# A mixture-of-experts kernel: a narrower all-token part of expert 0, its rows from one-hot products, and 64 slots on 64 array columns

## The chip, the cores and the metric

The kernel is written in Bass, with semaphores set by hand, and runs on one NeuronCore of a Trainium2 chip. The metric is the device time of one execution in microseconds (us).

## The reference

Two layers of an encoder on 256 tokens of 1024 values in float32. Each layer mixes tokens (one input projection; windowed attention on half of its columns, a pooling mixer on the other half; an output projection) and then channels. Layer 0 mixes channels with a dense SwiGLU, layer 1 with eight experts, of which each token takes two:

```python
D_MODEL, SEQ, DEPTH, D_FF, N_EXPERTS, TOP_K = 1024, 256, 2, 2816, 8, 2

def swiglu(t, w_gate, w_up, w_down):
    return (jax.nn.silu(t @ w_gate) * (t @ w_up)) @ w_down

def moe_swiglu(h, w_router, w_gate, w_up, w_down):
    t = h.reshape(B * S, Dm)
    logits = (t @ w_router).astype(jnp.float32)
    top_vals, top_idx = lax.top_k(logits, TOP_K)
    top_w = jax.nn.softmax(top_vals, axis=-1)
    gates = jnp.sum(jax.nn.one_hot(top_idx, N_EXPERTS) * top_w[..., None], axis=1)
    out = 0
    for e in range(N_EXPERTS):
        out = out + gates[:, e:e + 1] * swiglu(t, w_gate[e], w_up[e], w_down[e])
    return out

def reference(x, ...):
    for l in range(DEPTH):
        h = rms_norm(x, pre_mix_gain[l])
        y = ...                          # attention and pooling of h, times w_out[l]
        x = x + rms_norm(y, post_mix_gain[l])
        h = rms_norm(x, pre_ffn_gain[l])
        f_out = swiglu(h, ...) if l % 2 == 0 else moe_swiglu(h, ...)
        x = x + rms_norm(f_out, post_ffn_gain[l])
    return x
```

The expert weights are 8 x 3 x 1024 x 2816 values in float32, 277 MB; every expert is used, so all of them are read.

## The kernel before

**Experts.** The kernel computes an expert only for the tokens that chose it. Each expert has `SLOTS` = 96 slots for tokens: 64 form part A (`A_SLOTS`), 32 part B (`B_SLOTS`). The experts stand in an order of places p = 0 to 7; expert 0 is always at p = 0, the others are put in order by their number of tokens. `CAPS` gives each place 96 slots or 64: places 2 and 7 have part A alone (`has_b`). A round for tokens beyond the slots exists and is not entered with these inputs.

**TensorE in the expert stage.** The 2816 hidden columns of an expert are taken in three chunks c of 1024, 1024 and 768 columns (`width`, `col0`). The stationary operand is the tokens' rows (`xg`, turned so that the model dimension is on the partitions), the moving operand are the weights as they came from memory. A step of `gate_up` (L1996) is one k of eight: 128 rows of the gate or up weights times the width of the chunk. For part A it issues four matmuls on tiles of 128 rows and 32 columns of the array (L2011): two groups g of 32 slots, each with the two halves h of the chunk's columns. For part B it issues one matmul of 256 columns per 256 columns of the chunk (L2015), each on its own 32 array columns. `down` (L2041) has blocks of 128 hidden columns: four matmuls of 512 columns for A (L2064) and four of 256 for B (L2069), all on 32 array columns. So every matmul of both functions uses a tile `128*32`:

```python
for q in range(4):
    h, g = divmod(q, 2)
    last = pe.matmul(ps[tile(q), (B_GATE, B_UP)[part], 0:w // 2], xg[:, rows_at, k, tile(g)],
                     weights[:, h * w // 2:(h + 1) * w // 2], start=k == 0, stop=k == KT - 1)
if has_b(p):
    for q in range(w // FC):
        last = pe.matmul(ps[tile(q), (B_GATE_B, B_UP_B)[part], 0:FC], xg[:, rows_at, k, A_SLOTS:SLOTS],
                         weights[:, q * FC:(q + 1) * FC], start=k == 0, stop=k == KT - 1)
```

The order on TensorE is that of `experts` (L2102): for each place and chunk the gate steps, then the turning of the hidden rows of the chunk before (`turn_hidden`, L2026 for A and L2037 for B), the up steps, for c > 0 the turning of one half of the gathered rows of the next expert (`turn_picked`, L2099), and `down` of the chunk before. The turnings are transposes with an identity on TensorE. The last chunk's `down` follows behind early additions at the end.

**Loads.** SyncE's queue loads the weights in that order, in 280 pieces of up to 1 MB (`load_piece`: L831 for down, L836 for gate and up, two k to a piece) into a ring of 16 slots. A slot is loaded again when TensorE has counted the piece in it as used (`ring_used`). The first sixteen pieces take memory of the stages before: `RING_ORDER` lists the slots, and `first_use` (L808) what each waits for: the dense stage's down weights (n < 2), the attention (n < 4), the low parts of the first pieces (n < 8), then TensorE's last use of those pieces.

**Expert 0 in front.** So that TensorE has work while the tokens are routed, the first 512 hidden columns (`WIDE`) of expert 0 are computed for all 256 tokens. Their gate and up weights come in four pieces of two k (`load_first`, L799, `FIRST_PIECES`), each split by ScalarE and VectorE into a high and a low part (`split_first` at L1157 and L2283; for piece 2, `split_by_k`, L2275, in two halves). `all_piece(j, t)` (L1845) multiplies piece j with token tile t: for each of two k and of gate and up three products of 512 columns (`mm3`, L1541: high by high, low by high, high by low), so twelve matmuls a call, eight calls. `first_chunk` (L1866) sets the order: the products of token tile 0 (tokens 0 to 127), its router logits (`route`, L1813), the turning of the normalised rows of tile 1 (`turn_rows`, L1547, behind `post_norm` and `pre_norm` on VectorE, L2338 and L2310, and a square and a root on ScalarE), the router of tile 1 and the products of tile 1, with `find_places` (L1823) and `find_rows` (L1834) between them. VectorE turns the logits into one-hot matrices (`onehots`: token by slot). Expert 0's tokens then come in four steps: TensorE multiplies the one-hots with token numbers, VectorE copies the row (`tok_row`), GpSimdE gathers the rows from memory (`gather_picked`, L1050, out of `tok_dram`, where both tiles' rows were stored), and `turn_first` (L1882) turns them. `pick_hidden` (L1895) picks the hidden rows of expert 0's slots out of the all-token part by one-hot products on L1901, so that `down` of this part works on slots as elsewhere. The other 2304 columns of expert 0 are three chunks of 768.

The gather of a later place p + 2 waits until the rows of place p + 1 are turned. The space of the turned rows `xg` lies over `rows`, the normalised rows.

## Time and profile before

| what | value |
|---|---|
| three runs | 1048.09, 1048.44, 1050.11 us (median 1048.44) |
| profiled execution | 1048.1 us, span of its instructions 1046.3 us |
| TensorE clock granted, mean | 0.995 of full speed |
| instructions of TensorE | 9903 matmuls (transposes are matmuls too) |
| HBM read | 341 MB |
| layer 0 and the mixing of layer 1 | 0 to about 320 us |
| first steps on expert 0's slots | 364.6 us |

```text
span 1046.3 us, 22297 instructions
## 1 busy us (share of the span) xinstructions
PE 1022.9 (98%) x9903; PEld 578.9 (55%) x9903; DVE 270.5 (26%) x418; ACT 250.7 (24%) x426; POOL 54.3 (5%) x159
## 2 busy tenths in 40 slices
PE   8999999999999899999999999999999999999985
PEld 7987888888998654444433334444444444443321
DVE  7677545446677410000000000000000000000022
ACT  7766534344775200000000000000000000000021
POOL 4000000000101000001001000001001000100200
PEclk9999999999999999999999999999999999999998
DMA  8488556542638899999999999999999999999994
GB/s 290 175 264 275 195 175 201 186 160 97 213 112 299 293 366 361 420 418 359 397 420 408 419 418 408 418 419 401 399 419 419 402 419 419 406 418 418 418 406 166
DMA packets 125149, 347.24 MB, mean 332 GB/s; under 512 B 7368, under 2 KB 40176, under 8 KB 125056
## 3 DMA queue, kind: packets, MB, share of 16 engines
q1 hardware_dynamic: 119760, 331.64, 82.0%
q0 software_dynamic: 4560, 13.41, 3.8%
q8 instruction: 76, 1.25, 0.4%
q10 hardware_dynamic: 736, 0.80, 0.2%
q14 instruction: 17, 0.14, 0.0%
HBM read 341.10 MB, written 4.72 MB: 331 GB/s over the span
## 4 chain that ended last, share of the span: by engine, by line
PE 93%; DMA 3%; DVE 2%; issue 1%; SPq 1%; ACT 1%; DVEq 0%; ACTq 0%; POOLq 0%
PE ps L2011 29%; PE ps L2064 14%; PE ps L2015 10%; PE ps L1543 9%; PE ps L1545 9%; PE ps L1544 9%; PE ps L2069 5%; DMA ring<-in_moe_w_down 2%; PE ps L2026 1%; DMA gains<-tok_rows,tok_row 1%; PE ps L2099 1%; DMA raw_gu<-in_w_in 1%; SPq L831 0%; PE ps L1550 0%; PE ps L1932 0%
## 5 line engine op out<-in xcount | busy, mean ns | idle before, releaser
L2011 PE MATMUL ps<-ring,xg 128*32 128x512 f32 (+1 forms) x3072 | 380.0, 550 | 2.6 <-DMA ring<-in_moe_w_gate 1.6
L2064 PE MATMUL ps<-ring,moe_ht 128*32 128x512 f32 x1408 | 177.3, 593 | 2.7 <-DMA ring<-in_moe_w_down 2.7
L2015 PE MATMUL ps<-ring,xg 128*32 128x256 f32 x2048 | 176.2, 379 | 0.0
L2011 PEld LDWEIGHTS ps<-ring,xg 128*32 128x32 f32 x3072 | 110.6, 110 | 99.7 <-issue 47.3
L2015 PEld LDWEIGHTS ps<-ring,xg 128*32 128x32 f32 x2048 | 73.2, 110 | 146.6 <-issue 146.6
L1543 PE MATMUL ps<-hi_gu,xt_hi 128*128 128x512 f32 (+1 forms) x352 | 132.3, 376 | 1.3 <-DVE lo_gu L2257 1.1
L1545 PE MATMUL ps<-hi_gu,xt_lo 128*128 128x512 f32 (+1 forms) x352 | 129.1, 367 | 0.0
L1544 PE MATMUL ps<-lo_gu,xt_hi 128*128 128x512 f32 (+1 forms) x352 | 129.0, 367 | 0.0
L1438 ACT ACTIVATE moe_silu<-ps 128x512 f32<-128x512 f32 (+1 forms) x24 | 13.3, 553 | 333.8 <-PE ps L2015 275.3
L2701 DVE COPY moe_ht<-ps 128x256 f32<-128x256 f32 (+1 forms) x18 | 7.1, 394 | 295.5 <-PE ps L2037 295.5
L2069 PE MATMUL ps<-ring,moe_ht 128*32 128x256 f32 x1056 | 81.2, 379 | 0.0
L2711 DVE TENSOR_TENSOR moe_hidden<-moe_silu,ps 128x512 f32<-128x512 f32 (+1 forms) x24 | 15.2, 632 | 255.2 <-PE ps L2015 189.1
L2069 PEld LDWEIGHTS ps<-ring,moe_ht 128*32 128x32 f32 x1056 | 34.3, 110 | 79.0 <-issue 79.0
L1543 PEld LDWEIGHTS ps<-hi_gu,xt_hi 128*128 128x128 f32 x352 | 66.6, 189 | 13.6 <-issue 1.2
L1545 PEld LDWEIGHTS ps<-hi_gu,xt_lo 128*128 128x128 f32 x352 | 66.6, 189 | 11.1
L1544 PEld LDWEIGHTS ps<-lo_gu,xt_hi 128*128 128x128 f32 x352 | 66.7, 190 | 9.9
L2064 PEld LDWEIGHTS ps<-ring,moe_ht 128*32 128x32 f32 x1408 | 43.8, 110 | 50.8 <-issue 24.3
L2197 DVE TENSOR_TENSOR lo_gu<-raw_gu,hi_gu 128x2048 fp32r<-128x2048 f32 x24 | 54.7, 2283 | 2.9 <-ACT hi_gu L1100 2.1
L1456 ACT COPY xg<-ps 128x384 f32<-128x384 f32 (+1 forms) x16 | 7.2, 452 | 135.1 <-PE ps L2099 135.1
L1100 ACT CAST hi_gu<-raw_gu 128x2048 fp32r<-128x2048 f32 x20 | 38.2, 1908 | 0.0
L1058 POOL DMA_DIRECT2D y_rows<-y_sb x14 | 7.6, 545 | 580.7 <-ACT y_sb L1463 580.7
L2518 DVE TENSOR_TENSOR lo_d<-raw_d,hi_d 128x1024 fp32r<-128x1024 f32 x20 | 23.6, 1221 | 31.4 <-ACT hi_d L1377 31.4
(326 smaller groups left out, 879.5 us busy)
## 6 DMA issues: line engine op xcount, KB each, us to landing
ring<-in_moe_w_down SPq DMA_DIRECT2D x88, 1024.0 KB, 16.5
ring<-in_moe_w_gate SPq DMA_DIRECT2D x56, 1024.0 KB, 17.6
ring<-in_moe_w_up SPq DMA_DIRECT2D x56, 1024.0 KB, 17.9
ring<-in_moe_w_gate SPq DMA_DIRECT2D x40, 768.0 KB, 15.3
ring<-in_moe_w_up SPq DMA_DIRECT2D x40, 768.0 KB, 14.2
raw_gu<-in_dense_w_gate SPq DMA_DIRECT2D x22, 512.0 KB, 3.9
raw_gu<-in_dense_w_up SPq DMA_DIRECT2D x22, 512.0 KB, 4.9
raw_d<-in_dense_w_down SPq DMA_DIRECT2D x11, 1024.0 KB, 4.9
```

Source lines behind the costliest of these rows:

```text
L1100: act.copy(hi_gu[at], raw_gu[at]).then_inc(gu_hi_done, 1)
L1438: last = act.activation(moe_silu[:, 0:w // 2], ps[:, B_GATE, 0:w // 2], ACT.Silu)
L1543: pe.matmul(o, a_hi, b_hi, start=first, stop=False)
L1544: pe.matmul(o, a_hi, b_lo, start=False, stop=False)
L1545: return pe.matmul(o, a_lo, b_hi, start=False, stop=last)
L2011: last = pe.matmul(ps[tile(q), (B_GATE, B_UP)[part], 0:w // 2], xg[:, rows_at, k, tile(g)], weights[:, h * w // 2:(h + 1) * w // 2], start ...
L2015: last = pe.matmul(ps[tile(q), (B_GATE_B, B_UP_B)[part], 0:FC], xg[:, rows_at, k, A_SLOTS:SLOTS], weights[:, q * FC:(q + 1) * FC], start=k ...
L2064: last = pe.matmul(ps[tile(q), B_YA, :], moe_ht[:, at:at + 32], weights[:, h * 512:(h + 1) * 512], start=start, stop=stop)
L2069: last = pe.matmul(ps[tile(q), B_YB, 0:FC], moe_ht[:, at:at + 32], weights[:, q * FC:(q + 1) * FC], start=start, stop=stop)
L2197: dve.tensor_tensor(lo_gu[at], raw_gu[at], hi_gu[at].bitcast(F32), ALU.subtract).then_inc(gu_lo_done, 1)
L2518: dve.tensor_tensor(lo, raw_d[:, c % 2, k, :], hi.bitcast(F32), ALU.subtract).then_inc(d_lo_done, 1)
L2711: last = dve.tensor_tensor(moe_hidden[:, 0:w // 2], moe_silu[:, 0:w // 2], ps[:, B_UP, 0:w // 2], ALU.mult)
```

## The change

The part of expert 0 that is computed for all tokens has 256 hidden columns instead of 512. It comes in two pieces of four k, gate and up side by side in one product of 512 columns; pieces 2 and 3, their splits on ScalarE and VectorE and their loads are gone. The rest of expert 0 has chunks of 1024, 1024 and 512 columns; in the last, B's groups are 128 wide and a piece has four k. The two slots of memory that become free, and the four behind them, come earlier in `RING_ORDER`. Expert 0's rows are no longer gathered: `pick_rows` multiplies the rows of all tokens with the one-hot matrix on TensorE, which gives them turned at once. For this `xg` no longer lies over `rows`. Part A is issued as two matmuls on 64 array columns (`half_tile`), one for each half of the chunk's columns, instead of four on 32. Part B stays on 32.

```diff
-B_LOGITS, B_PLACES, B_COUNTS, B_ALL, B_XG0 = 4, 4, 7, ((0, 1), (5, 6)), (3, 7)
+B_LOGITS, B_PLACES, B_COUNTS, B_ALL, B_XG0 = 4, 4, 7, (0, 5), (3, 7)
...
-    FIRST_PIECES = 4
+    FIRST_PIECES = 2
...
-    RING_ORDER = [4, 5, 14, 15] + [first_slot(j) for j in range(FIRST_PIECES)] + \
+    EARLY_SLOTS = [first_slot(j) for j in range(FIRST_PIECES, 4)]
+    RING_ORDER = [4, 5, 14, 15] + EARLY_SLOTS + [base + n for n in EARLY_SLOTS for base in (6, 10)] + \
+        [first_slot(j) for j in range(FIRST_PIECES)] + \
         [base + first_slot(j) for j in range(FIRST_PIECES) for base in (6, 10)]
...
     def width(p, c):
 
         if c < 0:
-            return WIDE
-        return 3 * FC if p == 0 or c == CHUNKS - 1 else 4 * FC
+            return FC
+        if c < CHUNKS - 1:
+            return 4 * FC
+        return 3 * FC if p else 2 * FC
 
     def col0(p, c):
 
         if c < 0:
             return 0
-        return WIDE + c * 3 * FC if p == 0 else c * 4 * FC
+        return c * 4 * FC + (0 if p else FC)
+
+    def b_width(p, c):
+        return P if width(p, c) == 2 * FC else FC
+
+    def b_groups(p, c):
+        return width(p, c) // b_width(p, c)
+
+    def k_tiles(p, c):
+
+        return 2 if width(p, c) > 2 * FC else 4
+
+    def gate_pieces(p, c):
+        return KT // k_tiles(p, c)
...
         if c < 0:
             return b * SLOTS + A_SLOTS
-        q, j = divmod(b, 2)
+        q, j = divmod(b, b_width(p, c) // P)
         return 512 + j * P + q * B_SLOTS
...
+    def half_tile(h):
+        return slice(A_SLOTS * h, A_SLOTS * (h + 1))
...
-                to = flat_piece(raw_gu, slot).rearrange("p (k w c) -> p k w c", k=2, w=2)
+                to = flat_piece(raw_gu, slot).rearrange("p (k w c) -> p k w c", k=4, w=2)
                 for part, w in enumerate((moe_w_gate, moe_w_up)):
-                    sp.dma_start(to[:, :, part, :], w[0, 0][2 * j * P:(2 * j + 2) * P, 0:WIDE]
+                    sp.dma_start(to[:, :, part, :], w[0, 0][4 * j * P:(4 * j + 4) * P, 0:FC]
                                  .rearrange("(k p) n -> p k n", p=P)).then_inc(gu_loaded[slot // 2][slot % 2], 16)
 
             def first_use(n):
@@ -811,10 +828,14 @@
                     sp.wait_ge(d_lo_done, 2 * NCH)
                 elif n < 4:
                     sp.wait_ge(attn_mm, TT * DEPTH)
-                elif n < 8:
-                    sp.wait_ge(gu_lo_done, PIECE0 + n - 4 + 1)
...
+                elif n < 6:
+                    sp.wait_ge(gu_lo_done, PIECE0)
+                elif n < 10:
+                    sp.wait_ge(out_mm, TT * DEPTH)
+                elif n < 12:
+                    sp.wait_ge(gu_lo_done, PIECE0 + n - 10 + 1)
                 else:
-                    sp.wait_ge(first_used, (n - 8) // 2 + 1)
+                    sp.wait_ge(first_used, (n - 12) // 2 + 1)
...
                 else:
-                    w, c0 = width(p, c), col0(p, c)
-                    sp.dma_start(ring[:, slot, 0:2 * w].rearrange("p (k n) -> p k n", k=2),
-                                 expert_rows((moe_w_gate, moe_w_up)[part], e)[i * FC:(i + 1) * FC, c0:c0 + w]
+                    w, c0, kn = width(p, c), col0(p, c), k_tiles(p, c)
+                    sp.dma_start(ring[:, slot, 0:kn * w].rearrange("p (k n) -> p k n", k=kn),
+                                 expert_rows((moe_w_gate, moe_w_up)[part], e)[i * kn * P:(i + 1) * kn * P, c0:c0 + w]
                                  .rearrange("(k p) n -> p k n", p=P)).then_inc(ring_loaded[slot], 16)
...
             pool.wait_ge(tok_stored, 16 * TT)
             pool.wait_ge(tok_row_ready, 1)
-            gather_picked(0)
-            pool.wait_ge(tok_row_ready, 2)
-            pool.wait_ge(picked_turned, 2)
             gather_picked(1)
...
                 transposed(l, T_FFN, 0)
                 split_first(l, 1)
                 post_mix(l, 1)
-                split_first(l, 2)
                 pre_ffn(l, 1)
-                split_first(l, 3)
                 transposed(l, T_FFN, 1)
...
-            def all_piece(j, t, between=None):
+            def all_piece(j, t):
 
                 hi, lo = flat_piece(hi_gu, first_slot(j)), flat_piece(lo_gu, first_slot(j))
                 a = slice(t * P, (t + 1) * P)
-                for k in range(2):
-                    kt = 2 * j + k
-                    if (j, t, k) == (2, 0, 0):
-                        pe.wait_ge(first_k_lo, 1)
-                    elif t == 0:
-                        pe.wait_ge(gu_lo_done, PIECE0 + j + 1)
-                    if k and between:
-                        between()
-                    for part in range(2):
-                        at = slice((2 * k + part) * WIDE, (2 * k + part + 1) * WIDE)
-                        last = mm3(ps[:, B_ALL[t][part], :], xt_hi[:, kt, a], xt_lo[:, kt, a], hi[:, at], lo[:, at],
-                                   kt == 0, kt == KT - 1)
+                if t == 0:
+                    pe.wait_ge(gu_lo_done, PIECE0 + j + 1)
+                for k in range(4):
+                    kt, at = 4 * j + k, slice(k * WIDE, (k + 1) * WIDE)
+                    last = mm3(ps[:, B_ALL[t], :], xt_hi[:, kt, a], xt_lo[:, kt, a], hi[:, at], lo[:, at], kt == 0, kt == KT - 1)
                 if t == 1:
                     last.then_inc(first_used, 1)
-                elif j == 3:
+                elif j == FIRST_PIECES - 1:
                     last.then_inc(all_tile0, 1)
 
             def first_chunk():
                 all_piece(0, 0)
-                all_piece(1, 0)
                 pe.wait_ge(router_lo_done, 1)
                 route(0)
-                all_piece(2, 0)
                 turn_rows(1, T_FFN, 1)
-                all_piece(3, 0)
+                all_piece(1, 0)
                 xt_ready(1, T_FFN, 1)
                 route(1)
                 all_piece(0, 1)
                 find_places()
-                all_piece(1, 1, lambda: find_rows(0, range(1)))
-                all_piece(2, 1)
-                all_piece(3, 1, turn_first)
-
-            def turn_first():
-                pe.wait_ge(counted, 1)
+                all_piece(1, 1)
                 for part in range(2):
-                    turn_picked(0, part)
+                    pick_rows(part)
+
+            def pick_rows(part):
+                pe.wait_ge(*((counted, 1) if part else (onehots_ready, 1)))
+                for k in range(4):
+                    at = slice((part * 4 + k) * P, (part * 4 + k + 1) * P)
+                    for t in range(TT):
+                        last = pe.matmul(ps[:, B_XG0[part], k * SLOTS:(k + 1) * SLOTS], rows[:, t, at],
+                                         onehots[:, t, 0, 0:SLOTS].bitcast(F32), start=t == 0, stop=t == TT - 1)
+                last.then_inc(picked_turned, 1)
...
+                for k in range(2):
...
@@ -1998,23 +2009,24 @@
...
-                    pe.wait_ge(*((all_silu, 1) if part == GATE else (all_hidden, 1)))
+                    pe.wait_ge(all_hidden, 1 if part == GATE else TT)
...
+                kn = k_tiles(p, c)
                 for k in range(KT):
-                    slot = piece_ring(p, c, part, k // 2)
-                    if k % 2 == 0:
-                        pe.wait_ge(ring_loaded[slot], piece_level(p, c, part, k // 2, step))
-                    weights = ring[:, slot, (k % 2) * w:(k % 2 + 1) * w]
-                    for q in range(4):
-                        h, g = divmod(q, 2)
-                        last = pe.matmul(ps[tile(q), (B_GATE, B_UP)[part], 0:w // 2], xg[:, rows_at, k, tile(g)],
+                    slot = piece_ring(p, c, part, k // kn)
+                    if k % kn == 0:
+                        pe.wait_ge(ring_loaded[slot], piece_level(p, c, part, k // kn, step))
+                    weights = ring[:, slot, (k % kn) * w:(k % kn + 1) * w]
+                    for h in range(2):
+                        last = pe.matmul(ps[half_tile(h), (B_GATE, B_UP)[part], 0:w // 2], xg[:, rows_at, k, 0:A_SLOTS],
                                          weights[:, h * w // 2:(h + 1) * w // 2], start=k == 0, stop=k == KT - 1)
                     if has_b(p):
-                        for q in range(w // FC):
-                            last = pe.matmul(ps[tile(q), (B_GATE_B, B_UP_B)[part], 0:FC], xg[:, rows_at, k, A_SLOTS:SLOTS],
-                                             weights[:, q * FC:(q + 1) * FC], start=k == 0, stop=k == KT - 1)
-                    if k % 2:
+                        wb = b_width(p, c)
+                        for q in range(b_groups(p, c)):
+                            last = pe.matmul(ps[tile(q), (B_GATE_B, B_UP_B)[part], 0:wb], xg[:, rows_at, k, A_SLOTS:SLOTS],
+                                             weights[:, q * wb:(q + 1) * wb], start=k == 0, stop=k == KT - 1)
+                    if k % kn == kn - 1:
                         last.then_inc(ring_used, 1)
...
                     weights = ring[:, slot, (b % 2) * D:(b % 2 + 1) * D]
                     start, stop = first and b == 0, end and b == width(p, c) // P - 1
-                    for q in range(4):
-                        h, g = divmod(q, 2)
-                        at = a_at(p, c, b) + 32 * g
-                        last = pe.matmul(ps[tile(q), B_YA, :], moe_ht[:, at:at + 32], weights[:, h * 512:(h + 1) * 512],
+                    for h in range(2):
+                        at = a_at(p, c, b)
+                        last = pe.matmul(ps[half_tile(h), B_YA, :], moe_ht[:, at:at + A_SLOTS], weights[:, h * 512:(h + 1) * 512],
                                          start=start, stop=stop)
...
             def turn_picked(p, part):
-                b, cap = B_XG0[part] if p == 0 else B_XG, CAPS[p]
-                pe.wait_ge(picked_loaded, p * 16 + 16)
-                if p:
-                    pe.wait_ge(xg_ready, 2 * p + part)
-                    if has_b(p - 1):
-                        pe.wait_ge(ht_b_ready, b_chunk_of(p - 1, part) + 1)
+                cap = CAPS[p]
+                pe.wait_ge(picked_loaded, p * 16)
+                pe.wait_ge(xg_ready, 2 * p + part)
+                if has_b(p - 1):
+                    pe.wait_ge(ht_b_ready, b_chunk_of(p - 1, part) + 1)
                 for k in range(4):
                     at = slice((part * 4 + k) * P, (part * 4 + k + 1) * P)
-                    last = pe.transpose(ps[:, b, k * cap:(k + 1) * cap], picked[0:cap, at], ident[0:cap, 0:cap])
+                    last = pe.transpose(ps[:, B_XG, k * cap:(k + 1) * cap], picked[0:cap, at], ident[0:cap, 0:cap])
                 last.then_inc(picked_turned, 1)
...
             def split_first(l, j):
-                if l and j == 2:
-                    split_by_k(j)
-                elif l:
+                if l:
                     split_first_piece(j)
...
                 post_norm(l, POST_MIX, 1, banks(B_OUT[1], 2))
-                split_first(l, 2)
                 pre_norm(l, PRE_FFN, 1)
-                split_first(l, 3)
...
                 link(dve.tensor_scalar(slot[:], rank[:], NOT_CHOSEN, None, ALU.add))
-                dve.wait_ge(tok_row_mm, 1)
-                dve.tensor_copy(tok_row[:, 0:1], ps[:, B_PLACES, 8 * E:8 * E + 1]).then_inc(tok_row_ready, 1)
```

Left out are the same widths put into the copies, the SiLU and the products of the hidden rows, the memory of `xg`, and the counts of semaphores.

## Rows read from the trace of the kernel before

**Rows 1.** The page, busy time and instructions of each engine.

```profile
PE 1022.9 (98%) x9903; PEld 578.9 (55%) x9903; DVE 270.5 (26%) x418; ACT 250.7 (24%) x426; POOL 54.3 (5%) x159
```

**Rows 2.** Window; PE, PEld, DVE, ACT, POOL busy us; clock; DMA share; GB/s.

```profile
318.00:400.00 82.00, 77.96 (x647) 53.58 (x645) 32.74 (x71) 21.58 (x30) 3.60 (x5) 0.98 0.90 322
500.00:957.00 457.00, 457.00 (x5461) 188.60 (x5457) 21.42 (x46) 28.30 (x61) 17.98 (x31) 1.00 1.03 413
```

**Rows 3.** TensorE's timeline: start of a group, its length, line, form, records.

```profile
454.09 0.61 PE L2015 MATMUL ps<-ring,xg 128*32 128x256 f32 x8
454.63 0.55 PE L2026 MATMUL ps<-ident,moe_hidden 128*128 128x128 f32 x3
455.02 0.33 PE L2037 MATMUL ps<-ident,moe_hidden 96*128 96x96 f32 x2
455.28 1.06 PE L2011 MATMUL ps<-ring,xg 128*32 128x512 f32 x8
...
700.50 1.04 PE L2011 MATMUL ps<-ring,xg 128*32 128x512 f32 x8
701.36 0.61 PE L2015 MATMUL ps<-ring,xg 128*32 128x256 f32 x8
701.79 1.04 PE L2011 MATMUL ps<-ring,xg 128*32 128x512 f32 x8
```

**Rows 4.** The chain from 995 us to the end, in order of time.

```profile
1001.48 0.95 SPq L836
...
1008.04 16.74 DMA ring<-in_moe_w_down
...
1029.08 5.33 PE ps L2064 x48
```

**Rows 5.** The windows view, a stretch of layer 0's dense stage.

```profile
100.00:150.00 50.00, 50.00 (x228) 41.37 (x227) 24.87 (x21) 20.98 (x21) 0.00 (x0) 1.00 0.63 201
```

**Rows 6.** Around the first experts' start: timelines, one step of chain, one window.

```profile
335.60 2.35 DVE L2281 TENSOR_TENSOR lo_gu<-raw_gu,hi_gu 128x1024 fp32r<-128x1024 f32 x2
338.06 1.28 DVE L2310 SCALAR_TENSOR_TENSOR rows<-x_res,rstd,gains 128x1024 f32<-128x1024 f32 x1
...
344.97 0.11 PE ps L1820
...
360.79 1.47 PE L2099 MATMUL ps<-ident,gains 96*128 96x96 f32 x8 [3.98 <-DMA gains<-tok_rows,tok_row]
...
360.80:364.30 3.50, 3.50 (x14) 2.97 (x14) 0.00 (x0) 0.96 (x2) 0.00 (x0) 0.51 1.03 417
...
374.92 2.00 PE L1901 MATMUL ps<-onehots,y_sb 128*128 128x96 f32 x16
```

**Rows 7.** Durations by line (ns: least, median, most), first and last start.

```profile
L2011 PE MATMUL ps<-ring,xg x3072: 485/592/617, 364.6 to 1015.9; 128*32 128x512 f32 x112, 128*32 128x384 f32 x80
...
L1698 PE MATMUL ps<-k_t,q_t x64: 269/269/320, 35.7 to 291.1; 64*64 64x128 f32 x64
...
L2026 PE MATMUL ps<-ident,moe_hidden x86: 272/273/330, 400.2 to 1027.0; 128*128 128x128 f32 x86
```

**Rows 8.** TensorE's timeline in the attention of layer 1, columns as in rows 3.

```profile
289.81 0.50 PE L1693 MATMUL ps<-k_t,q_t 64*128 64x128 f32 x6
290.24 0.45 PE L1698 MATMUL ps<-k_t,q_t 64*64 64x128 f32 x8
...
305.51 0.22 PE L1717 MATMUL ps<-v_mid,probs 128*64 128x65 f32 x1
305.57 0.22 PE L1717 MATMUL ps<-v_mid,probs 128*64 128x65 f32 x1
```

**Rows 9.** Groups by line and form: busy us, mean ns; idle before.

```profile
L2015 PE MATMUL ps<-ring,xg 128*32 128x256 f32 x2048 | 176.2, 379 | 0.0
L2069 PE MATMUL ps<-ring,moe_ht 128*32 128x256 f32 x1056 | 81.2, 379 | 0.0
```

More of the change, by code:

```diff
@@ L177, in build_trunk @@
             for part in (GATE, UP):
-                for i in range(4):
+                for i in range(gate_pieces(p, c)):
                     PIECE[p, c, part, i] = len(PIECE)
@@ L214, in piece_level @@
         if slot < 4:
-            earlier = first_level([first_slot(j) for j in range(FIRST_PIECES)].index(slot))
+            earlier = first_level([first_slot(j) for j in range(4)].index(slot) - (4 if slot in EARLY_SLOTS else 0))
         else:
@@ L224, in last_piece @@
     def last_piece(p, c, part, step=None):
-        i = 3 if part != DOWN else width(p, c) // FC - 1
+        i = gate_pieces(p, c) - 1 if part != DOWN else width(p, c) // FC - 1
         return piece_number(p, c, part, i, step) + 1
@@ L872, in _ @@
                     for part in (GATE, UP):
-                        for i in range(4):
+                        for i in range(gate_pieces(p, c)):
                             if (p, c, part) != (0, 0, GATE) or i >= 2:
@@ L1439, in silu_of @@
                 if has_b(p):
-                    some = b_rows(p, c)
-                    last = act.activation(moe_silu[some, 512:3 * FC], ps[some, B_GATE_B, 0:FC], ACT.Silu)
+                    some, wb = b_rows(p, c), b_width(p, c)
+                    last = act.activation(moe_silu[some, 512:512 + wb], ps[some, B_GATE_B, 0:wb], ACT.Silu)
                 last.then_inc(silu_ready, 1)
@@ L1450, in copy_picked_ht @@
                 act.wait_ge(hidden_picked, 1)
-                act.copy(moe_ht[:, 0:4 * SLOTS], ps[:, B_HTA, 0:4 * SLOTS]).then_inc(picked_ht_ready, 1)
+                act.copy(moe_ht[:, 0:2 * SLOTS], ps[:, B_HTA, 0:2 * SLOTS]).then_inc(picked_ht_ready, 1)
             def copy_xg(p, part):
@@ L1832, in find_places, with find_rows @@
                 last.then_inc(counts_mm, 1)
-            def find_rows(n, some):
-                pe.wait_ge(onehots_ready, n + 1)
-                for e in some:
+            def find_rows():
+                pe.wait_ge(onehots_ready, 2)
+                for e in range(1, E):
                     for t in range(TT):
@@ L1897, in pick_hidden @@
                 pe.wait_ge(all_hidden, TT)
-                for k in range(4):
+                for k in range(2):
                     at = slice(k * P, (k + 1) * P)
@@ L2035, in turn_hidden @@
                     some = b_rows(p, c)
-                    for j in range(2):
+                    for j in range(b_width(p, c) // P):
                         last = pe.transpose(ps[:, B_HTB, j * P:j * P + some.stop], moe_hidden[some, 512 + j * P:512 + (j + 1) * P],
@@ L2045, in down @@
                     pe.wait_ge(picked_ht_ready, 1)
[L2046 removed]
+                    pe.wait_ge(tok_row_ready, 1)
                 else:
@@ L2108, in experts @@
                         if (p, c) == (0, 0):
-                            find_rows(1, range(1, E))
+                            find_rows()
                             pick_hidden()
@@ L2273, in copy_q @@
                                   ).then_inc(q_copied, 1)
-            def split_by_k(j):
-                slot_at = first_slot(j)
-                dve.wait_ge(gu_hi_done, PIECE0 + j + 1)
-                for k in range(2):
-                    raw, hi, lo = (flat_piece(ring, slot_at)[:, k * 2 * WIDE:(k + 1) * 2 * WIDE] for ring in (raw_gu, hi_gu, lo_gu))
-                    dve.tensor_tensor(lo, raw, hi.bitcast(F32), ALU.subtract).then_inc(gu_lo_done if k else first_k_lo, 1)
             def split_first(l, j):
-                if l and j == 2:
-                    split_by_k(j)
-                elif l:
+                if l:
                     split_first_piece(j)
```

34 lines of the change are left out of this document (16 added, 18 removed).

## The prediction

> **What bounds the kernel now.** I first read the page's busy shares and then one table over time. TensorE is busy 98% of the span [rows 1]. From 500 to 957 us it has no idle time, while the DMA engines are full at 413 GB/s [rows 2], so the expert stage is held from two sides at nearly the same rate. One step of the stage (128 rows of gate or up weights, 1024 columns) takes 0.86 us for the first 64 slots (part A, L2011) and 0.43 us for the other 32 (part B, L2015) [rows 3]. That is 1.29 us, or 2.58 us for the two steps that use up one piece of 1.05 MB, which is 407 GB/s. TensorE is the slower side, by 1.5%. The two experts without a part B need 1.72 us for a piece and live on what the ring holds. For the last of them that does not suffice: the chain is TensorE's until 1001 us and then goes over the issue of the last transfers and a transfer of 16.74 us [rows 4].
>
> How much do these waits cost? From 1001.25 us, TensorE's remaining work is 16 steps of 768 columns (0.86 x 3/4 = 0.645 us), four pieces of down weights at 1.72, turns and early additions of 3.1, and the last three pieces in 5.33 [rows 4]: 25.7 us, to 1026.95. It really ends at 1034.4. So 7.4 us are DMA waits, which vanish if TensorE becomes slower before that point.
>
> **The change, part by part.** *Narrower all-token part.* For each token tile, each of four pieces was a block of 12 products, 50/228 = 0.22 us apart [rows 5]; here, with small gaps, I take 0.23, so 2.75 us a block. Only two pieces are left. I count from the rows of token tile 1, which both kernels need. VectorE ends them at 339.34 us, behind two subtractions of 2.35 us that the change removes [rows 6]. What then holds is ScalarE's square and root of that tile, and 0.65 us of the 2.35 are gained: 338.7. Before, the experts begin at 364.6 [rows 7], 25.3 us after the rows. After, TensorE does from 338.7 on: eight turns at (455.02 - 454.63)/3 = 0.13 [rows 3], 1.0, three blocks 8.25, 16 router and 5 place products at 0.11 [rows 6] = 2.3, and the new one-hot products, and then waits for one copy of 0.65 us that nothing hides. The new products have the form of L1901 (16 records in 2.00 us [rows 6], 0.112 apart): 32 records, 3.6 us. Together 15.8, so the experts begin at 354.5. I take 354.6, 10.0 us earlier. Gone from the 25.3 us are two blocks, the wait of 3.98 us for the gathered rows and their turning in 1.47 [rows 6], and what the half clock behind that wait costs (granted 0.51, the lower of the two levels, 1.2 GHz [rows 6]). Picking the hidden rows halves (1.0 us less). The 14 records that find the other experts' rows stay.
>
> There is a price in front: TensorE, through with its first block and the router at about 334.9, waits for the rows until 338.7. An idle stretch of 3.98 us was followed by half the clock [rows 6], so 3.8 us may be too. Bound: 0 to 1.8 us; I take 0, since it would fall partly under the following chain on ScalarE and VectorE.
>
> *Columns moved.* Expert 0 had 48 gate/up steps of 768 columns, 0.645 + 0.43 = 1.075 us each: 51.6 us. Now it has 32 of 1024 (1.29) and 16 of 512 (0.43 + 0.215): 51.6 us. The down blocks are 22 in both. This costs nothing. The bytes are the same as well: 2.1 MB move from the first loads to the ring.
>
> *Loads.* On SyncE's queue the two freed slots and the four behind them open early, so up to 8 MB can be under way before 340 us. DMA moves 322 GB/s from 318 to 400 us and 413 when it is full [rows 2]. Hence it has room for 82 x (1 - 322/413) = 18 us of transfers and can follow a gain of 11 us. GpSimdE's queue loses one gather, and the one for expert 1 no longer waits for expert 0's turning: needed at about 400 us, hidden either way. In sum so far: -11.0 us.
>
> *64 columns of the array at once.* Part A goes from four matmuls on 32 array columns to two on 64. Four streams of 512 columns side by side take 0.86 us; two streams of the same length take the same if two really run together. They do: on tiles 128*64, pairs start 0.06 us apart for 65 columns [rows 8], which is one stream's time for two. So A itself gains nothing. But B stays on tiles 128*32. Before, A and B had one form; now each step changes form twice.
>
> What a change of form costs is in the trace. The last B record ends at 454.70 and lasts 379 ns [rows 9], so it starts at 454.32; it streams 0.213 us, to 454.535, and the first record of the form 128*128 starts at 454.63. The way back is the same: the last turn ends at 455.35 and, with 96 columns, lasts 0.25 (273 ns for 128 columns [rows 7], less 0.03 of streaming), so it starts at 455.10 and streams 0.08, and the form 128*32 starts at 455.28 [rows 3]. A third change alters only the array's columns, from 64*128 to 64*64: the last pair (end 290.31, length 0.27) starts at 290.04 and streams 0.107, the next starts at 290.24 [rows 8]. Each leaves 0.095 us empty. Then the weights are loaded in sight: the first records last 617 instead of 592 ns for 32 columns, and 320 instead of 269 for 64 [rows 7], so 0.025 and 0.051. Third, everything waits for the last of the side-by-side tiles, which start 0.007 us apart: 0.02 with four, 0.007 with two. Hence A to B costs 0.127 us and B to A 0.166.
>
> How often? Six of the eight experts have a part B, each with 48 gate/up steps and 22 down blocks: 420 steps (L2069's 1056 records are 132 blocks of eight [rows 9]; L2015's 2048 belong to 288 steps). So 420 times A to B is 53.3 us. B to A is 389 times, 64.6 us, because 31 steps (18 gate chunks before a turn of hidden rows, 12 up chunks before a turn of gathered rows, one before the last one-hots) end before work on 128 columns, where the change exists already. Another 40 returns from such work go to 64 columns instead of 32, 1.0 us. Together 119 us, all on TensorE, which is the bound here.
>
> No row changes between 64 and 32 columns, so the bounds are wider: below, no cost at all; above, the dearest change seen (at 454.63: 0.54 us after 454.09 where a B group takes 0.43 [rows 3], so 0.11 late, and 330 instead of 273 ns [rows 7] for the load, 0.06: 0.17) each time, 138 us. I take 119, since the nearest row, 64*128 to 64*64, also changes columns alone. The Trainium skill has a rule on this ("TensorEngine Tiling (Array Packing)", Key Properties): changing the tiling mode, not just the tile, drains TensorE. By that rule the 119 us come; the same list says that different tiles load and multiply in parallel, and if that covered tiles of two widths they would not.
>
> **The sum.** Span 1046.3 - 11.0 (first part) - 7.4 (waits at the end that go) + 119 = 1147 us. Around the span lie 1.8 us (1048.1 less 1046.3), so 1148.7, say **1149 us**. The profiled execution is 0.3 us below the median of 1048.44. What becomes late next is nothing but TensorE: at 1.29 + 0.293 = 1.58 us a step a piece lasts 3.2 us against 1.05/0.413 = 2.5 for its transfer, and the ring is full when each narrow expert starts.
>
> **The rivals.**
> *No cost of the change of form.* If tiles of 64 and 32 columns share the array as tiles of one width do, only the 11 us remain. Then DMA sets the end as now, but started earlier: 1048.1 - 11 = 1037 us. For it: column tiles overlap freely within one form. Against it: all forms that follow each other in the trace leave 0.095 us. It decides from 11 + 7.4 us of added TensorE time, 0.044 us a step: below that the kernel is faster. Chance 0.12.
> *Only the loads are exposed.* The array isn't emptied, but weights of another width can't be loaded ahead: 420 x 0.025 + 389 x 0.051 + 1 = 31 us. TensorE is the bound, 1048.1 - 18.4 + 31 = 1061 us. For it: the loads of 454.63 are not pulled ahead. Against it: they come 0.095 us after the stream, not at once. Chance 0.07.
> *Cost in full*, the forecast: 0.80. What is left, 0.01, is no change.
>
> **How the numbers follow.** The forecast's own range: 809 changes at the bare 0.095 us are 77 us, which gives 1107; at 0.171 us they are 138, which gives 1168; the clock in front adds up to 1.8. So 1106 to 1168, and this already holds 8 in 10; the two rivals lie outside. Differences within 0.2% are about what can't be told from none here: same 0.02, faster 0.12, slower 0.86.
>
> **What the profile should show.** Forecast: L2011 and L2064 as 128*64 with half the records (1536 and 704), and a step of 1.58 us where it was 1.29; idle gaps on TensorE with no releaser, about 0.1 us, twice a step; DMA below 350 GB/s in the steps of B experts; experts starting near 354.6 us; DMA no longer in the chain's end. The gather's wait of 3.98 us is gone, and an idle stretch of about 3.8 us stands near 335. I am wrong if the step stays at 1.29 us (then 1037), or if a step of A alone, in the experts without B, is not 0.86 us, which would mean that two tiles of 64 don't run together for 512 columns.

## The result, and the profile after

The changed kernel takes 1149.51 us (median of 4 runs, 1148.61 to 1150.95) against 1048.26 us before in the same comparison: a ratio of 1.0965, 95% interval 1.0947 to 1.0982. The forecast was 1149. The profiled execution is the longest of the four, 1150.95 us with a span of 1148.3. One of the six executions of e4_group_all below had a granted clock of 0.942, where all others had 0.99 or more, and took 1074.8 us; it is left out of every comparison.

Of the page, busy time by engine [rows 1], the lines for part A and part B, and the last line of TensorE in the chain:

```profile
PE 1129.0 (98%) x7725; PEld 510.9 (44%) x7725; DVE 265.6 (23%) x414; ACT 246.7 (21%) x424; POOL 53.3 (5%) x158
...
L2022 PE MATMUL ps<-ring,xg 128*64 128x512 f32 (+2 forms) x1536 | 364.9, 572 | 0.6 <-ACT xg L1472 0.6
L2075 PE MATMUL ps<-ring,moe_ht 128*64 128x512 f32 x704 | 181.3, 611 | 0.0
L2027 PE MATMUL ps<-ring,xg 128*32 128x256 f32 (+1 forms) x2144 | 180.1, 385 | 0.0
...
L2080 PE MATMUL ps<-ring,moe_ht 128*32 128x256 f32 x1056 | 84.3, 391 | 0.0
```

Part A (L2022, L2075) has half the records that it had before (L2011, L2064), and TensorE is busy for 106 us longer. It is 98% busy before and after: the share says nothing here, since the roughly 0.1 us in which nothing streams at a change lie inside the duration of the last records (a record of 256 columns lasts 0.379 us and streams for 0.213). One has to look at the starts. TensorE's timeline of one step in expert 0, to be read against [rows 3]:

```profile
359.97 1.08 PE L2022 MATMUL ps<-ring,xg 128*64 128x512 f32 x4
360.98 0.64 PE L2027 MATMUL ps<-ring,xg 128*32 128x256 f32 x8
361.55 0.65 PE L2022 MATMUL ps<-ring,xg 128*64 128x512 f32 x2
```

A takes 360.98 - 359.97 = 1.01 us where it took 0.86, B 0.57 where it took 0.43. The step is 1.58 us, as forecast, against 1.29. What a record lasts shows the part of it that is weight loading: the durations (least, median, most) of the two lines are

```profile
L2022 PE MATMUL ps<-ring,xg x1536: 379/592/644, 358.4 to 1121.6; 128*64 128x512 f32 x128, 128*64 128x384 f32 x56, 128*64 128x256 f32 x8
...
L2027 PE MATMUL ps<-ring,xg x2144: 272/379/403, 359.4 to 1052.1; 128*32 128x256 f32 x184, 128*32 128x128 f32 x11
```

The median of both is that of before, 592 and 379 ns. Only the longest, those behind a change, last 0.052 and 0.024 us more. There the new weights are not loaded ahead: the loads for this B begin at 360.97 us, together with its first product at 360.98, while in the kernel before the loads for the B group at 454.09 us began at 453.66. In an expert without part B nothing changes width, and there the wide tiles cost nothing. The timeline has one such group (its first record may lie outside the window):

```profile
600.41 3.17 PE L2022 MATMUL ps<-ring,xg 128*64 128x512 f32 x13
```

Thirteen records are six pairs and one. Less the 0.59 of the last record, six pairs start in 2.58 us, 0.43 a pair, 0.86 for the two pairs of a step.

The windows, to be read against [rows 2] and the last view of [rows 6]:

```profile
336.70:340.40 3.70, 0.12 (x2) 0.03 (x1) 2.12 (x3) 1.45 (x3) 0.53 (x1) 0.68 1.02 417
340.60:344.80 4.20, 4.20 (x14) 3.71 (x15) 1.19 (x1) 2.21 (x2) 0.54 (x1) 0.50 1.01 340
344.90:350.80 5.90, 5.90 (x35) 5.13 (x34) 2.07 (x9) 0.30 (x2) 0.00 (x0) 1.00 1.01 395
500.00:957.00 457.00, 457.00 (x3302) 120.24 (x3298) 18.33 (x39) 24.79 (x53) 14.00 (x24) 1.00 0.97 358
```

From 500 to 957 us TensorE again has no idle time, but the DMA engines move 358 GB/s instead of 413, because the slots of the ring come free later: SyncE's queue waits for TensorE in 333 of these 457 us, where it was 134. From 400 to 500 us, where both experts have a part B, it is 306 GB/s (forecast: below 350). In front of the experts TensorE is idle for 3.7 us, and the clock then stands at 0.50 (1.2 GHz) until about 344.8. The waits say what it was idle for; no wait for a transfer is left in the list, where before there were 2.7 us at L2064 alone:

```profile
PE ps L1566 <- DVE rows L2310: 3.7, 1, 3.7
...
PE ps L2022 <- ACT xg L1472: 0.6, 1, 0.6
```

### The profile page after: what moved, and what is told of

Same layout as the page of the kernel before. It is cut to its first block, busy times and chain, and to the rows that moved or that the text cites. A ratio compares the mean times of both kernels' runs of the same rounds, so it can differ in the third digit from the quotient of the medians.

```text
span 1148.3 us, 17922 instructions
## 1 busy us (share of the span) xinstructions
PE 1129.0 (98%) x7725; PEld 510.9 (44%) x7725; DVE 265.6 (23%) x414; ACT 246.7 (21%) x424; POOL 53.3 (5%) x158
## 4 chain that ended last, share of the span: by engine, by line
PE 94%; DVE 2%; DMA 2%; ACT 1%; issue 1%; SPq 0%; DVEq 0%; ACTq 0%
PE ps L2022 30%; PE ps L2075 15%; PE ps L2027 14%; PE ps L1559 8%; PE ps L1561 7%; PE ps L1560 7%; PE ps L2080 7%; DMA raw_gu<-in_w_in 2%; PE ps L2038 1%; PE ps L2109 1%; PE ps L1566 1%; PE ps L1943 0%; PE ps L1733 0%; PE ps L1752 0%; PE ps L1741 0%
## 5 line engine op out<-in xcount | busy, mean ns | idle before, releaser
L2022 PE MATMUL ps<-ring,xg 128*64 128x512 f32 (+2 forms) x1536 | 364.9, 572 | 0.6 <-ACT xg L1472 0.6
L2075 PE MATMUL ps<-ring,moe_ht 128*64 128x512 f32 x704 | 181.3, 611 | 0.0
L2027 PE MATMUL ps<-ring,xg 128*32 128x256 f32 (+1 forms) x2144 | 180.1, 385 | 0.0
L2022 PEld LDWEIGHTS ps<-ring,xg 128*64 128x64 f32 x1536 | 83.8, 135 | 157.3 <-issue 155.9
L2027 PEld LDWEIGHTS ps<-ring,xg 128*32 128x32 f32 x2144 | 44.8, 108 | 209.8 <-issue 209.8
L1454 ACT ACTIVATE moe_silu<-ps 128x512 f32<-128x512 f32 (+2 forms) x24 | 13.4, 558 | 404.5 <-PE ps L2027 341.4
L2698 DVE COPY moe_ht<-ps 128x256 f32<-128x256 f32 (+2 forms) x18 | 7.2, 398 | 360.5 <-PE ps L2049 360.5
L2708 DVE TENSOR_TENSOR moe_hidden<-moe_silu,ps 128x512 f32<-128x512 f32 (+2 forms) x24 | 15.3, 638 | 291.2 <-PE ps L2027 228.9
L2075 PEld LDWEIGHTS ps<-ring,moe_ht 128*64 128x64 f32 x704 | 38.6, 135 | 74.2 <-issue 72.7
L2080 PEld LDWEIGHTS ps<-ring,moe_ht 128*32 128x32 f32 x1056 | 20.8, 108 | 107.1 <-issue 107.1
```

Source lines behind the costliest of these rows:

```text
L1454: last = act.activation(moe_silu[:, 0:w // 2], ps[:, B_GATE, 0:w // 2], ACT.Silu)
L2022: last = pe.matmul(ps[half_tile(h), (B_GATE, B_UP)[part], 0:w // 2], xg[:, rows_at, k, 0:A_SLOTS], weights[:, h * w // 2:(h + 1) * w // 2] ...
L2027: last = pe.matmul(ps[tile(q), (B_GATE_B, B_UP_B)[part], 0:wb], xg[:, rows_at, k, A_SLOTS:SLOTS], weights[:, q * wb:(q + 1) * wb], start=k ...
L2075: last = pe.matmul(ps[half_tile(h), B_YA, :], moe_ht[:, at:at + A_SLOTS], weights[:, h * 512:(h + 1) * 512], start=start, stop=stop)
L2080: last = pe.matmul(ps[tile(q), B_YB, 0:FC], moe_ht[:, at:at + 32], weights[:, q * FC:(q + 1) * FC], start=start, stop=stop)
L2708: last = dve.tensor_tensor(moe_hidden[:, 0:w // 2], moe_silu[:, 0:w // 2], ps[:, B_UP, 0:w // 2], ALU.mult)
```

## The experiments

Ten kernels ran. The first four were compared with each other and with before (median 1048.37) on one chip.

**Part A back on 32 columns (e1_a32).** The inverse of the diff's edit in `gate_up` and `down`, all else as changed:

```diff
-                    for h in range(2):
-                        last = pe.matmul(ps[half_tile(h), ...], xg[:, rows_at, k, 0:A_SLOTS],
+                    for q in range(4):
+                        h, g = divmod(q, 2)
+                        last = pe.matmul(ps[tile(q), ...], xg[:, rows_at, k, tile(g)],
```

> The changed kernel with part A back on four matmuls on 128*32 tiles; everything else of the change stays (256 all-token columns, one-hot products for the rows, chunks of 1024, 1024, 512, the earlier loads). Theory (each change of the tile's width costs 0.10 us on TensorE before and about 0.04 us behind it, nothing else of the change costs): the step is 1.29 us again and the whole added time of 108 us in the expert stage goes; the front part keeps its gain, of which about 2 us are eaten by the half clock behind the idle stretch at 337 us, so 1037 to 1041 us. Rival (the loss comes from the new chunks, the piece of four k or the loads at SyncE): it stays well above 1048 us, at 1060 to 1149 us.

Measured: 1039.09 us (1037.67 to 1043.82), ratio to before 0.9924, interval 0.9895 to 0.9952. The 64-column tiles alone cost 110.4 us, more than the whole loss of 101.3, and the rest of the change gains 9 us. Its chain, in order of time from 330 us on, has the transfers of [rows 4] back:

```profile
993.42 1.57 SPq L852
995.18 1.59 SPq L852
996.96 16.74 DMA ring<-in_moe_w_down
1013.74 1.92 PE ps L2077 x16
1017.98 5.33 PE ps L2077 x48
```

**The kernel before with part A on 64 columns (e2_before_a64).** The same edit the other way round, in the kernel before.

> The kernel before with one edit: part A as two matmuls on 128*64 tiles. Same columns, loads, gather. Theory: the same 420 changes 64 to 32 and 389 back, 0.288 us a step: step 1.575 us, plus 117 us, less the 7.4 us of transfer waits near the end that it covers: 1156 to 1161 us. Rival (two wide tiles are cheap and the loss lies elsewhere in the change): 1048 us or a little less.

Measured: 1157.43 us (1156.96 to 1160.25), ratio 1.1043, interval 1.1019 to 1.1067, so 109.1 us more. Both ways the price of the tiles is the same within 1.3 us, hence it doesn't come from the new chunks, the loads or the front.

**Fewer changes of width (e3_group_piece).** In the changed kernel the products stay the same and only their order changes. `group` is the number of k that one piece holds, for `down` two blocks:

```diff
-                for k in range(KT):
...
+                for k0 in range(0, KT, group):
+                    for b_part in range(2 if has_b(p) else 1):
+                        for k in range(k0, k0 + group):
```

> The changed kernel with the same products in another order: within each loaded piece all of part A first, then all of part B, so the width changes twice a piece instead of twice a step. Theory (the price hangs on the number of changes): changes 64 to 32 fall from 420 to 206, changes back from 389 to 175, 62 us less: 1085 to 1090 us, two steps in 2.87 us. Rival (a product on a 128*64 tile or the narrow product beside it is itself slower): unchanged, 1149 us. Rival (only the weight loads show): the same fall of about half, but without the empty 0.1 us at each remaining change.

Measured: 1088.4 us (1087.34 to 1089.2), 61.1 less. The timeline of one piece:

```profile
361.07 1.94 PE L2031 MATMUL ps<-ring,xg 128*64 128x512 f32 x8
362.94 1.07 PE L2027 MATMUL ps<-ring,xg 128*32 128x256 f32 x16
363.94 1.94 PE L2031 MATMUL ps<-ring,xg 128*64 128x512 f32 x8
```

Two steps in 2.87 us, as expected: A has 1.87 against 1.72, B 1.00 against 0.86. The excess at each change is what it was, 0.15 and 0.14 us; there are half as many. The fall of 61.1 us over 214 pairs of changes is 0.286 us for a pair. That this 0.14 to 0.15 us remains at each change refutes the rival by which only the loads show (0.024 and 0.052 us).

**All of A, then all of B (e4_group_all).** `group` is the whole chunk.

> The changed kernel with all of part A of a chunk's gate, up or down first and then all of part B: 55 changes 64 to 32 and 24 back are left. Theory: 107 us less by TensorE's count, 1042 us; a piece is given back only in the part B pass, so the ring holds up to four pieces longer and the DMA engines, which then bound the stage, may lose some: 1040 to 1050 us. Rival (price not by the number of changes): near 1149 us.

Measured: 1045.51 us (median of five executions, 1044.57 to 1046.82), ratio 0.9961, interval 0.9942 to 0.998. With 420 - 55 = 365 and 389 - 24 = 365 changes fewer each way, 0.286 us a pair make 104.4; measured are 104.0. Three points (0, 214 and 365 pairs fewer) lie on one line. TensorE's waits on transfers are only 0.7 us, so holding the ring's slots longer cost next to nothing. My 1042 was low since I had used 0.293 a pair.

**Two widths on separate columns (e9_mixed_halves, with e10_one_width_halves as control).** Does a change wait only where the new tile lies over a busy one? Here each wide product on one half of the array is followed by narrow ones on the other half. The wide product behind them then lies on the same columns as they do, so that the run answers the question for the step from 64 columns to 32, not for the way back.

```diff
                     for h in range(2):
...
-                    if has_b(p):
...
-                        for q in range(b_groups(p, c)):
...
+                        if has_b(p):
...
+                            for q in range(2 * (1 - h), min(2 * (2 - h), b_groups(p, c))):
...
```

> The changed kernel with the gate and up products of a step in the order: part A's first half of columns on array columns 0 to 63 (tile 128*64), part B's groups on columns 64 to 127 (tiles 128*32), part A's second half on 64 to 127, part B's groups on 0 to 63. down is as in the changed kernel. The two widths never want the same array columns at the same time. Theory (a change of width empties the whole array, wherever the tiles lie): the four phases of a step run one after the other, 0.86 + 0.43 + 0.86 + 0.43 = 2.58 us and four changes of 0.144, 3.15 us a step; with 344 us of added streaming and 83 us of added changes, 1576 us. Rival (only tiles that overlap wait for each other, so tiles of two widths run side by side): the step falls towards 1.3 to 1.7 us and the time to 1066 to 1180 us.

> The same order of halves as in e9_mixed_halves, but part A on tiles 128*32 throughout, as a control: one width, no change. It shows what the order itself costs. If tiles of one width run freely beside each other, a step takes 1.29 us (each half of the array has 0.86 + 0.43 us of work) and the time is 1039 us; if the queue hands them out strictly in order, so that a second pass on a tile holds those behind it, up to 1.72 us a step, 1039 + 288 x 0.4 = 1155 us; if neighbouring groups don't overlap at all, 2.58 us, 1390 us.

Measured: 1566.88 us for the two widths and 1039.88 us for the control in one run each, beside 1045.76 for the kernel before. The timeline with two widths:

```profile
403.31 1.07 PE L2022 MATMUL ps<-ring,xg 128*64 128x512 f32 x2
404.31 0.63 PE L2027 MATMUL ps<-ring,xg 128*32 128x256 f32 x4
404.87 1.07 PE L2022 MATMUL ps<-ring,xg 128*64 128x512 f32 x2
405.87 0.62 PE L2027 MATMUL ps<-ring,xg 128*32 128x256 f32 x4
406.43 1.07 PE L2022 MATMUL ps<-ring,xg 128*64 128x512 f32 x2
```

and the same order with one width:

```profile
403.20 0.39 PE L2028 MATMUL ps<-ring,xg 128*32 128x256 f32 x2
403.22 0.60 PE L2023 MATMUL ps<-ring,xg 128*32 128x512 f32 x2
403.42 0.39 PE L2028 MATMUL ps<-ring,xg 128*32 128x256 f32 x2
403.63 0.60 PE L2023 MATMUL ps<-ring,xg 128*32 128x512 f32 x2
403.65 0.60 PE L2028 MATMUL ps<-ring,xg 128*32 128x256 f32 x4
404.06 0.61 PE L2023 MATMUL ps<-ring,xg 128*32 128x512 f32 x4
```

Each product is two records (part A's 768 products in `gate_up` are L2022's 1536 records), called its first and second pass here. With one width the first pass of B (403.20) and the second pass of A (403.22) start together, by the order of the program on different halves, and the step is 1.29 us. With two widths the phases follow one another, 1.56 us each (403.31 to 404.87), two a step: 3.12 us. The narrow products at 404.31 and 405.87 us do not wait for their own columns: those were free during the whole wide product before. So at a change from 64 columns to 32 nothing starts before the wide products are through, wherever the tiles lie. That the same holds from 32 to 64 is not shown by this run; the change costs about as much either way (0.15 and 0.14 us above). This is the rule that the prediction cited from the Trainium skill ("TensorEngine Tiling (Array Packing)", Key Properties): changing the mode, not just the tile, drains TensorE. The 1576 us of the expectation follow from it; this case's trace agrees as far as it goes, with 1566.9 us and 3.12 us a step where 3.15 were expected. The other line of that list in the Trainium skill, that different tiles load and multiply in parallel, holds here within one width, where the control's step is 1.29 us.

The next four were compared on one chip with before at 1047.77 us. The base:

> The kernel of e1_a32 once more, as the base that the next three are compared with on one chip: 1039 us, as there.

Measured: 1039.27 us (1038.09 to 1041.44), ratio 0.9926, interval 0.9913 to 0.9939.

**Filling the idle stretch (e6_a32_fill).** `fill` issues 15 products of `xt_hi[:, 0, 0:P]` by 512 columns of piece 0 into the bank `B_UP`, which is not in use yet.

```diff
                 route(0)
+                fill(15)
                 turn_rows(1, T_FFN, 1)
```

> e1_a32 with 15 products of 512 columns into an unused bank in the place where TensorE waits 3.7 us for the rows of tile 1; the reference needs none of them. Theory (that idle stretch is what halves the clock for 6.8 us behind it): the granted clock stays at its full level from 337 us on, the eight turns take 0.9 instead of 1.97 us and the five or six products behind them 0.23 instead of 0.43, so the experts begin 2.2 us earlier and the time falls by as much, to 1036.5 to 1037.5 us. Rival (the clock falls for another reason, or the transfers set the end and take the 2 us back): 1039 us.

Measured: 1036.94 us (1036.38 to 1038.23), ratio 0.9901, interval 0.9887 to 0.9916. The windows before and behind the arrival of the rows:

```profile
335.00:338.70 3.70, 3.70 (x17) 2.72 (x16) 2.12 (x3) 1.45 (x3) 0.54 (x1) 1.00 1.02 418
338.90:343.00 4.10, 4.10 (x25) 3.60 (x25) 1.23 (x1) 2.30 (x2) 0.54 (x1) 1.00 1.03 344
```

and the timeline, turning and the first expert step:

```profile
338.89 1.10 PE L1566 MATMUL ps<-ident,rows 128*128 128x128 f32 x8 [0.18 <-DVE rows L2319]
...
354.72 1.06 PE L2030 MATMUL ps<-ring,xg 128*32 128x512 f32 x8 [0.57 <-ACT xg L1472]
```

The clock stays at full. The turning begins at 338.89 us, exactly as in the profile of e1_a32 (338.89), and the experts at 354.72 instead of 357.11: 2.4 us from the clock alone, and the time falls by 2.3. The seven profiled executions with this front and the idle stretch have 17.39 to 18.57 us from the turning to the experts, this one 15.83, so the half clock costs 1.6 to 2.7 us.

**The one-hot products alone (e7_before_onehot_rows),** put into the kernel before:

```diff
             def turn_first():
-                pe.wait_ge(counted, 1)
                 for part in range(2):
-                    turn_picked(0, part)
+                    pick_rows(part)
```

with the memory of `xg` moved and expert 0's gather, number product and copy left out, as in the change.

> The kernel before with one part of the change alone: expert 0's rows from one-hot products on TensorE instead of the gather and the turning; still 512 all-token columns in four pieces, chunks of 768, part A on 32 columns. Theory: the wait of 4.0 us, the turning of 1.5 and about 1.0 of half clock behind the wait go, 3.6 us of products come: the experts begin 2.9 us earlier, 1045 to 1046.5 us. The narrower all-token part and the earlier loads are then worth the other 6 us of the 9 that e1_a32 gained. Rival (the gather was hidden for the most part, and the products only add): 1048 to 1052 us.

Measured: 1044.64 us (12 runs, 1042.8 to 1048.2), ratio 0.9971, interval 0.996 to 0.9983: 3.1 us less, 0.4 below the expected range. The experts begin at 361.25 us instead of 364.6, 3.3 us earlier (expected 2.9). The clock behind the products, where [rows 6] had 0.51:

```profile
355.00:361.00 6.00, 6.00 (x45) 5.49 (x43) 0.61 (x4) 0.96 (x2) 0.00 (x0) 1.00 1.02 408
```

So 3.1 of the 8.5 us that e5_a32_again gains come from the rows. The rest is put down to the narrower part and the earlier loads, which were not run alone.

**The front packed more closely (e8_best).** `all_piece(1, 0)` in two halves around the turning, with 9 and 4 filling products, and `pick_rows` ahead of the last k of `all_piece(1, 1)`:

```diff
+                all_piece(1, 0, range(2))
+                fill(9)
                 turn_rows(1, T_FFN, 1)
-                all_piece(1, 0)
+                all_piece(1, 0, range(2, 4))
+                fill(4)
...
-                all_piece(1, 1)
+                all_piece(1, 1, range(3))
                 for part in range(2):
                     pick_rows(part)
+                all_piece(1, 1, range(3, 4))
```

> e6_a32_fill with the first half of the second all-token piece of tile 0 moved into the idle stretch, the fill cut to nine products there and four behind the other half, and the one-hot products put ahead of the last k of tile 1's second piece, so that ScalarE's copy of the rows lies under three products. Theory: 0.35 us less before the router of tile 1 and 0.57 us less before the experts: 0.9 us below e6_a32_fill, 1035.5 to 1036.5 us. Rival (the transfers near the end take it back): the time of e6_a32_fill.

Measured: 1036.93 us (1035.83 to 1037.45), ratio 0.9898, interval 0.9883 to 0.9912. From the turning to the experts it is shorter, as the timeline shows:

```profile
339.65 1.10 PE L1566 MATMUL ps<-ident,rows 128*128 128x128 f32 x8 [0.18 <-DVE rows L2324]
...
354.73 1.06 PE L2035 MATMUL ps<-ring,xg 128*32 128x512 f32 x8
```

15.08 us against 15.83, and the wait of 0.57 is gone. The time is not the expected 1035.5 to 1036.5 but that of e6_a32_fill. In this profiled execution the rows came 0.76 us later, so that the experts begin at the same moment, 354.73 against 354.72 us, and the last transfer of the chain too (996.50 against 996.59). Four runs with a spread of 1.6 us don't resolve 0.75, and whether the transfers would take it back stays open.

## Why the prediction was right, and where it was not

**The bound.** TensorE and the transfers at nearly the same rate: confirmed. With one width the last transfers end the chain (16.74 us in e1_a32); with 117 us added to TensorE no wait for a transfer is left, so the 7.4 us at the end went as forecast. The kernel before with part A on 64 columns shows the sum of the two by itself, +109.1 us against the 117 - 7.4 expected for that run.

**The price of a change.** Priced from three changes of other forms, with 0.127 and 0.166 us, 0.293 a pair. Measured: 0.286. The loading in sight, taken as 0.025 and 0.051 us, is 0.024 and 0.052 in the durations; the rest is 0.21 of a pair, where the forecast had 0.217: twice 0.095 in which nothing streams, and 0.027 for the offset between side-by-side tiles. How the 0.21 divides between these two was not measured apart. The count, 420 and 389, was right by the fall of 61.1 and 104.0 us when 214 and 365 pairs were taken out. From the first expert step to the last product of `down` the profiled executions have 1034.41 - 364.6 = 669.8 us and 1136.59 - 358.39 = 778.2, 108.4 more, where the sum had 119 - 7.4 - 1.0 = 110.6. At 0.286 instead of 0.293 a pair the 119 are 116.2, 2.8 less, which covers that difference of 2.2.

**The wide tiles themselves.** Two side by side run as fast as four of half the width, 0.86 us a step in the experts without part B. That costs nothing and gains nothing: a record has a median of 592 ns with either width, and those side by side overlap. This sign, named in the forecast, came out as it said.

**The front.** I had the experts 15.8 us behind the rows, 354.6 us. The trace has 358.39. Of the 3.8 us, 1.8 lie ahead of the rows: VectorE's `post_norm` of tile 1 begins at 334.94 us instead of 333.14. The lag is there whole at 45 us already, in layer 0 (L2400 at 45.23 us instead of 43.43), and doesn't grow. At least half of it is scatter: the nine profiled executions with the new front have `post_norm` at 332.76 to 335.19 us, 334.0 in the mean, the three with the old one at 332.91 to 333.20. Whether the change itself adds the 0.9 us between the means stays open. The other 2.0 are the step that failed: the half clock behind the idle stretch. I forecast the idle stretch (3.8 us; measured 3.7) and took its price as 0, bound 1.8, because I thought it would fall partly under the chain of ScalarE and VectorE. It did not: TensorE turned the rows at half clock on that chain and then ran five products at 0.43 us. Filled, the stretch gives back 2.3 us; that and the 2.0 here are over my bound of 1.8. With it filled the experts stand 15.8 us behind the turning's start, which is what the products, the turning and the copy were added up to.

**The sum.** 1148.7 forecast for the profiled execution, 1150.95 measured: +1.8 for the lag from layer 0, +2.0 for the clock, -2.2 for the price of the changes, +0.9 for what lies around the span (2.65 instead of 1.8), -0.2 behind the last `down`. The mechanism, the count and the price within 3% were right; that the forecast is within 0.5 us of the median, 1149.51, is luck, since the clock and the price were off by 2 us in opposite directions.

**The rivals.** No cost (1037 us): refuted, since the wide tiles add 110.4 and 109.1 us in the two kernels. Loads alone (31 us): refuted; they are about a quarter of the price (0.076 of 0.286), and the rest remains at every change. Columns moved and loads: nothing, since e1_a32 has 1039.09 us, which is 1048.4 - 11 + 2.

## What to carry to other kernels

Count changes of the tile's shape like instructions: here a change of its columns costs 0.14 to 0.15 us, and a step of 1.29 us with two of them takes 22% longer, while the busy share doesn't move. If one operand needs another width, either bring all products to one width, or do all of one width first; splitting 64 columns into two tiles of 32 was free. An idle stretch ahead of a critical chain can have a second price, the half clock behind it; here products into an unused bank removed it.

The best version was the changed front with part A on 32 columns and the filling products: 1036.9 us, 1.0% below the kernel before.

## What the runs showed of the hardware

- A change from 64 columns to 32 waits for the wide products, even where the next product's columns are idle: 3.12 us a step against 1.29 for the same order in one width. For the way back this was not separated.
- Within one width, products on different columns need not wait for the second pass of an earlier one: in the control B's first pass starts at 403.20 us, the second pass of the part A product issued before it at 403.22. I had allowed 1.72 us a step for strict order; it was 1.29.
- 3.7 us of idle TensorE cost another 1.6 to 2.7 us afterwards, at a granted clock of 0.50; in the kernel before, the wait for the gathered rows had done the same (0.51), and both went when the wait went.
